# S5's order beside the input projection, and attention's values once a head

## The reference

```python
def s5_mixer(u, ...):
    lam_bar = jnp.exp(lam * dt)
    b_bar = ((lam_bar - 1.0) / lam)[..., None] * b
    bu = jnp.einsum('bsgh,gph->bsgp', uf.astype(jnp.complex64), b_bar)
    _, xs = lax.associative_scan(comb, (a, bu), axis=1)
    y = jnp.einsum('bsgp,ghp->bsgh', xs, c).real + d_skip * uf
    g = jax.nn.gelu(y)
    out = g * jax.nn.sigmoid(g @ w_glu + b_glu)

def block(args):        # attention: queries in blocks of 128, 4 heads
    s = jnp.einsum('bqhcd,bkhcd->bhcqk', qi, k) * scale
    s = jnp.where(kpos[None, :] <= qpos[:, None], s, -jnp.inf)
    p = jax.nn.softmax(s, axis=-1)
    a = p[:, :, 0] - lam * p[:, :, 1]
    return jnp.einsum('bhqk,bkhe->bqhe', a, v)
```

## Time and profile before

| | us |
|---|---|
| median of 3 runs | 1374.37 (1372.64 to 1374.88) |
| profiled execution, its own time | 1373.18 |
| its span | 1371.4 |
| TensorE busy | 1316.9 (96%) |
| TensorE weight loads busy | 1065.1 (78%) |
| VectorE busy | 849.8 (62%) |
| ScalarE busy | 500.6 (37%) |
| GpSimd busy | 612.7 (45%) |

### The profile page before, as it was taken

The page is one execution under the profiler, slowest core; times in us unless marked ns, Lnnn a source line. Parts: engine busy times, 40 slices in busy tenths (PEclk is TensorE's granted clock), DMA queues, the critical chain, the costliest instruction groups (busy, mean ns, idle before and its releaser), DMA issues.

```text
span 1371.4 us, 16028 instructions
## 1 busy us (share of the span) xinstructions
PE 1316.9 (96%) x6234; PEld 1065.1 (78%) x6234; DVE 849.8 (62%) x1149; ACT 500.6 (37%) x752; POOL 612.7 (45%) x288
## 2 busy tenths in 40 slices
PE   7988999999999999999999799989999999999999
PEld 4767777677888888888877687767778888888887
DVE  7847964656788406776237397646577771277731
ACT  5442355555323212322334234555552332122320
POOL 2966533124444444444468474312254444344442
PEclk9999999999999999999999999999999999999999
DMA  6321232013223322323233112311133333223332
GB/s 212 93 62 40 79 94 81 24 39 108 92 93 108 111 87 86 100 92 101 100 100 99 47 48 79 116 36 47 41 113 98 102 109 106 77 92 93 110 111 87
DMA packets 40939, 120.49 MB, mean 88 GB/s; under 512 B 6432, under 2 KB 10656, under 8 KB 40864
## 3 DMA queue, kind: packets, MB, share of 16 engines
q1 hardware_dynamic: 40864, 119.46, 27.3%
HBM read 114.20 MB, written 2.10 MB: 85 GB/s over the span
## 4 chain that ended last, share of the span: by engine, by line
PE 80%; DVE 9%; ACT 3%; issue 2%; SPq 2%; POOL 2%; DMA 1%; DVEq 0%; POOLq 0%; ACTq 0%
PE bank L492 25%; PE bank L505 23%; PE bank L497 23%; SPq L331 1%; PE bank L494 1%; PE bank L727 1%; PE bank L686 1%; POOL wl L353 1%; PE bank L706 1%; DVE bank L1376 1%; PE bank L716 1%; DVE xl L1137 1%; DVE G L1162 1%; ACT wh L863 1%; DMA raw<-in_w_in 1%
## 5 line engine op out<-in xcount | busy, mean ns | idle before, releaser
L353 POOL TENSOR_TENSOR wl<-raw,wh 128x1024 fp32r<-128x1024 f32 (+3 forms) x208 | 501.9, 2414 | 692.8 <-ACT wh L863 437.2
L863 ACT ACTIVATE wh<-raw 128x1024 fp32r<-128x1024 f32 (+3 forms) x208 | 218.6, 1051 | 283.9 <-PE bank L497 229.0
L492 PE MATMUL bank<-xl,wh 128*128 128x512 f32 x1152 | 308.2, 406 | 2.8 <-DVE xl L1137 2.2
L505 PE MATMUL bank<-xh,wl 128*128 128x512 f32 x1152 | 286.4, 390 | 0.0
L497 PE MATMUL bank<-xh,wh 128*128 128x512 f32 x1120 | 276.8, 389 | 0.0
L492 PEld LDWEIGHTS bank<-xl,wh 128*128 128x128 f32 x1152 | 216.7, 190 | 61.8 <-issue 12.9
L505 PEld LDWEIGHTS bank<-xh,wl 128*128 128x128 f32 x1152 | 215.4, 188 | 45.0 <-issue 0.3
L497 PEld LDWEIGHTS bank<-xh,wh 128*128 128x128 f32 x1120 | 210.2, 188 | 44.1
L1180 DVE TENSOR_TENSOR x<-x,bank 128x512 f32<-128x512 f32 x64 | 44.0, 687 | 225.3 <-PE bank L505 225.3
L492 PE MATMUL bank<-ml,wh 128*128 128x512 f32 x512 | 140.3, 402 | 0.0
L505 PE MATMUL bank<-mh,wl 128*128 128x512 f32 x512 | 127.4, 389 | 0.0
(11 more groups left out here) (292 smaller groups left out, 1271.4 us busy)
## 6 DMA issues: line engine op xcount, KB each, us to landing
raw<-in_w_gu SPq DMA_DIRECT2D x88, 512.0 KB, 3.5
raw<-in_w_in SPq DMA_DIRECT2D x52, 512.0 KB, 3.6
raw<-in_w_dn SPq DMA_DIRECT2D x32, 704.0 KB, 4.0
raw<-in_w_oe SPq DMA_DIRECT2D x16, 384.0 KB, 3.0
raw<-in_w_ol SPq DMA_DIRECT2D x16, 256.0 KB, 2.6
x<-in_x SPq DMA_DIRECT2D x8, 256.0 KB, 6.5
raw<-in_w_first SPq DMA_DIRECT2D x4, 512.0 KB, 4.8
out_x<-x SPq DMA_DIRECT2D x8, 256.0 KB, 4.5
```

The lines of the kernel that those rows point to most:

```text
L353: tt(wl[:, p, 0:cols], raw[:, p, 0:cols], wh[:, p, 0:cols].bitcast(F32), ALU.subtract).then_inc(wl_full, 1)
L492: mm(bank[b][:, :], wh[:, p, k * P:(k + 1) * P], lo[:, k, :], start=(k == 0), stop=False)
L505: w = mm(bank[b][:, :], wl[:, p, k * P:(k + 1) * P], hi[:, k, :], start=False, stop=(k == K - 1))
L863: fn(wh[:, p, 0:cols], raw[:, p, 0:cols], ACT.Copy).then_inc(wh_full, 1)
```

## The change

Units: before u (0, 1), xbc (2 to 7), z (8, 9); after z, xbc, u. S5's work follows: the input transposes in another order, the windows' copies in the tiles at MIXC of mh, without the wait for the states; the first half's input product behind unit 11, its output and the second half's input behind unit 16, the second half's output behind unit 22; VectorE's rotation and scan of a half are separate steps; GELU once for both halves at step 26. The exponentials of m2 stand behind the last SiLU. Attention: the transposed probabilities of a head are gathered by key block in `turned` (in the room of xh), and attend(h) makes four products, key block k with all queries from block k on; scores(n) is one product for each softmax.

The diff, cut to its core:

```diff
+        turned = [sb(f"turned{i}", [P, NQ, T], at=offsets["xh"] + i * NQ * T * 4) for i in range(2)]
-        local = [sb(f"s5_local{i}", [P, 4, P], at=offsets[n]) for i, n in enumerate(("bmat", "cf"))]
+        local = [sb(f"s5_local{i}", [P, 4, P], at=offsets["mh"] + (MIXC + i) * T * 4) for i in range(2)]
...
-                if s == 5:
-                    sp.wait_ge(unit_out, unit_out_of(l, 1))
-                if 5 <= s <= 8:
+                if 11 <= s <= 14:
+                    i = (s - 11) // 2
+                    if s % 2:
+                        sp.wait_ge(unit_out, unit_out_of(l, 8 + i))
...
-                if s in (17, 18, 21, 22):
+                if s in (20, 21, 25, 26):
...
-                    if 6 <= s <= 7:
-                        table(l, 0, s - 6)
-                    if 8 <= s <= 11:
-                        for n in ((0,), (1, 2), (3,), (4, 5))[s - 8]:
+                    if 6 <= s <= 8:
+                        state_terms(l, s - 6)
+                    if 9 <= s <= 10:
+                        table(l, 0, s - 9)
+                    if 11 <= s <= 12:
+                        for n in ((3, 4), (5,))[s - 11]:
                             state_terms(l, n)
...
             def s5_windows(l, i):
                 pe.wait_ge(kernels_copied, l + 1)
-                if i:
-                    pe.wait_ge(states_ready, 2 * (l + 1))
                 claim(6, local_copied)
...
-                if q:
-                    for c, b in enumerate(banks):
-                        mm(bank[b][:, 0:q * P], qs[c], qk[rows[c], 2 * h + 1, 0:q * P], start=True, stop=True)
                 for c, b in enumerate(banks):
-                    mm(bank[b][:, last], qs[c], qk[rows[c], 2 * h + 1, last], start=True, stop=False)
+                    w = (q + 1) * P
+                    mm(bank[b][:, 0:w], qs[c], qk[rows[c], 2 * h + 1, 0:w], start=True, stop=False)
...
-            def attend(l, n):
-                h, q = n // NQ, n % NQ
+            def attend(l, h):
...
-                pe.wait_ge(probs_turned, nth(probs_turned))
-                for k in range(q + 1):
-                    w = mm(bank[5][:, q * P:(q + 1) * P], v[:, k, h * P:(h + 1) * P],
-                           G[:, 4 + n % 2, k * P:(k + 1) * P], start=(k == 0), stop=(k == q))
+                pe.wait_ge(probs_turned, nth(probs_turned, NQ))
+                for k in range(NQ):
+                    w = mm(bank[5][:, k * P:], v[:, k, h * P:(h + 1) * P], turned[h % 2][:, k, k * P:],
+                           start=(k == 0), stop=(k == NQ - 1))
...
-                    if n:
-                        attend(l, n - 1)
+                    if n and n % NQ == 0:
+                        attend(l, n // NQ - 1)
...
-                attend(l, STEPS - 1)
+                attend(l, HEADS - 1)
...
                 for s in range(1, NIN):
                     prep()
+                    if 7 <= s <= 10:
+                        s5_inputs((1, 2, 4, 5)[s - 7])
...
+                    if s in (17, 23):
+                        y_copy((s - 17) // 6)
...
-                    if s in (20, 24):
-                        gelu((s - 20) // 4)
+                    if s == 26:
+                        gelu(0)
+                        gelu(1)
+                        ln_exp_tables()
...
-                        s5_scan(l, 0)
...
+                        s5_rotate(l, 0, 0)
+                        s5_rotate(l, 0, 1)
...
-                        s5_scan(l, 1)
+                        s5_scan(l, 0)
...
-                        s5_back(l, 1)
+                        s5_back(l, 0)
...
+                    if 17 <= s <= 18:
+                        s5_rotate(l, 1, s - 17)
+                    if 19 <= s <= 20:
+                        s5_scan(l, 1, [s - 19])
+                    if s == 21:
+                        s5_back(l, 1)
+                    if s in (21, 25):
+                        s5_finish(l, (s - 21) // 4)
...
-    order = [w[:, :, s5:z], w[:, :, xbc:dt], w[:, :, z:xbc], w[:, :, sc + 256:sc + 512], w[:, :, sc + 512:s5],
+    order = [w[:, :, z:xbc], w[:, :, xbc:dt], w[:, :, s5:z], w[:, :, sc + 256:sc + 512], w[:, :, sc + 512:s5],
```

More of the change, by code:

```diff
@@ L764, in _ @@
                         dt_turn()
[L765 to L766 removed]
+                    if s in (6, 8):
+                        s5_inputs(l, (0, 3)[(s - 6) // 2])
                     if s == 7:
@@ L791, in _ @@
                         m2_decays(3)
+                    if s == 16:
                         s5_out(l, 0)
-                    if s == 16:
+                        s5_in(l, 1)
                         m2_norm()
[L795 to L798, removed]
                     if 17 <= s <= 24:
@@ L970, in _ @@
                     prep()
[L971 to L975, removed]
+                    if 7 <= s <= 10:
+                        s5_inputs((1, 2, 4, 5)[s - 7])
+                    if s == 11:
+                        for i in range(2):
+                            s5_weights(local[i][:].rearrange("p a b -> p (a b)"), bank[6][:, :], local_copied)
+                    if s in (15, 21):
+                        s5_copy((s - 15) // 6)
+                    if s in (17, 23):
+                        y_copy((s - 17) // 6)
                     if s == 2:
@@ L986, in _ @@
                         fn(s16[:, 7, :], s16[:, 5, :], ACT.Exp).then_inc(decay_exp, 1)
[L987 to L991, removed]
+                    if l == 0 and s == 9:
+                        act.wait_ge(lam_go, 1)
+                        fn(lam2[:, :, :], lam2[:, :, :], ACT.Exp).then_inc(lam_exp, 1)
+                    if s == 10:
                         m2_head(0)
@@ L1348, in lambda_factors, with s5_rotate, s5_scan @@
                 own(tt(mlam_all[:, :], mlam_all[:, :], pre[:, :, PRE["linit"]].rearrange("p a b -> p (a b)"), SUB))
-            a5, c5, e5 = [t[:, :] for t in (sA, sC, sE)]
-            def s5_scan(l, j):
+            a5, c5, e5 = [t[:, :] for t in (sA, sE, sE)]
+            def s5_rotate(l, j, part):
                 cs, sn = [t[:, :] for t in tab[j]]
-                dve.wait_ge(tab_full, nth(tab_full))
-                dve.wait_ge(dve_bank[2], nth(dve_bank[2]))
-                dve.wait_ge(dve_bank[3], nth(dve_bank[3]))
-                if l or j:
-                    dve.wait_ge(s5x_ready, 2 * l + j)
-                re, im = bank[2][:, :], bank[3][:, :]
-                own(tt(a5, re, cs, MUL))
-                own(tt(c5, im, cs, MUL))
-                dve.wait_ge(dve_own, owned() - 1)
-                own(tt(re, re, sn, MUL))
-                dve.wait_ge(dve_own, owned() - 1)
-                own(tt(im, im, sn, MUL))
-                dve.wait_ge(dve_own, owned() - 1)
-                own(tt(re, c5, re, SUB))
-                dve.wait_ge(dve_own, owned() - 1)
-                own(tt(im, a5, im, ADD))
-                for back, rows in ((1, re), (0, im)):
-                    dve.wait_ge(dve_own, owned() - back)
+                re, im = bank[2][:, :], bank[3][:, :]
+                if part == 0:
+                    dve.wait_ge(tab_full, nth(tab_full))
+                    dve.wait_ge(dve_bank[2], nth(dve_bank[2]))
+                    dve.wait_ge(dve_bank[3], nth(dve_bank[3]))
+                    if l or j:
+                        dve.wait_ge(s5x_ready, 2 * l + j)
+                    own(tt(a5, re, cs, MUL))
+                    own(tt(c5, im, cs, MUL))
+                    dve.wait_ge(dve_own, owned() - 1)
+                    own(tt(re, re, sn, MUL))
+                else:
+                    dve.wait_ge(dve_own, owned())
+                    own(tt(im, im, sn, MUL))
+                    own(tt(re, c5, re, SUB))
+                    dve.wait_ge(dve_own, owned() - 1)
+                    own(tt(im, a5, im, ADD))
+            def s5_scan(l, j, parts=(0, 1)):
+                re, im = bank[2][:, :], bank[3][:, :]
+                for rows in [(re, im)[k] for k in parts]:
+                    dve.wait_ge(dve_own, owned())
                     for k in range(4):
@@ L1554, in _ @@
                 for i in range(2):
-                    scaled(u[:, i, :].rearrange("p (t c) -> p c t", t=CH), i, "p (c t) -> p c t", t=CH)
+                    scaled(z[:, i, :], i)
                 dt_scaled()
@@ L1574, in _ @@
                         lambdas()
-                    if l == 0 and s == 9:
+                    if l == 0 and s == 10:
                         lambda_factors()
@@ L1578, in _ @@
                         m2_sums()
-                    if s == 7:
+                    if 8 <= s <= 9:
+                        i = s - 8
+                        scaled(u[:, i, :].rearrange("p (t c) -> p c t", t=CH), i, "p (c t) -> p c t", t=CH)
+                    if s == 8:
                         m2_weights()
@@ L1600, in _ @@
                         m2_mix(1)
-                        s5_back(l, 0)
+                        s5_rotate(l, 0, 0)
+                        s5_rotate(l, 0, 1)
                     if 12 <= s <= 13:
```

92 lines of the change are left out of this document (40 added, 52 removed).

## The result

| | before | after |
|---|---|---|
| median us (4 runs each) | 1374.11 (1372.64 to 1374.88) | 1352.83 (1350.01 to 1354.09) |
| profiled execution, own time / span | 1373.18 / 1371.4 | 1352.78 / 1350.8 |
| TensorE busy | 1316.9 (96%) | 1310.9 (97%) |

Ratio 0.9851, 95% interval 0.9839 to 0.9864: 21 us faster, where 26.6 were forecast (1347.8 from 1374.4); 1352.83 lies in the range. First the chain by engine and TensorE's waits in total, as in the earlier trace rows.

The account below looks back on a forecast made before the run. TensorE was taken to bound the kernel, so only its work and gaps count. 1373.2 - 30.5 (input projection) + 3.9 (y copies) + 0 (attention) = 1346.6 us, 1347.8 against the median of 1374.4; range 1339 to 1359 for 8 in 10.

Parts of the forecast that it names:

- L574: S5's windows, input projection: dropping the wait for the states removes 11.5 us of waits and 5.3 of slow clock, 16.8 us.
- L551 and L562: S5's input transposes and kernels: reordered ScalarE copies remove 13.1 us of waits and about 3 of slow clock, 16 us.
- The vector chain: Units 11 to 16: VectorE becomes late, 2 us at second m2_apply and 0.8 at s5_out(0) a layer, 5.6 us added.
- A in all: First S5 transposes to start of unit 17: 30.5 us booked as removed, including 3.3 us beyond the named gaps.
- The y copies: Units 17 to 27: copies delay partner rows, 3.8 us a layer added, 3.7 us relief; net 3.9 us added.
- Attention, 0: Attention: wider value products and moved cover cancel to 0 a layer, bounds -1.5 and +2.5 us.
- SP's chunk copies at nothing: Loads of units 12 to 15: 32 DMAs copying u into chunks delay them, costed at nothing because the double buffer covers.
- the vector chain's clock at the y gap: Vector-chain rival: 2.8 + 4 us more, the y gap's lower clock adding 2 to 3; 1355 us, chance 0.17.
- the free y copies: Rival, units 17 to 27: partner rows arrive in time or copies go faster; -7.6 us, 1340 us, chance 0.12.
- the surviving wait: Rival, S5's windows: the wait is for local_copied or bank 6 and stays; +16.8 us, 1365 us, chance 0.04.
- the wide products: Rival, attention values: wide products are cheaper by the Trainium skill's rule, 10.7 us in all; 1337 us, chance 0.02.
- the slow SP: Rival: chunk copies hold up loads of units 12 to 15, 39.5 us over two layers; 1387 us, chance 0.04.

Follow-up runs that it names:

- windows_free: Kernel before with only the wait of S5's second window for the states removed, copies and the rotation's second buffer placed elsewhere: ratio 0.9868, 1354.08 us.
- copy_first: Changed kernel with ScalarE's copy of S5's input group 0 moved ahead of the SiLU of step 6: ratio 0.9867, 1354.73 us.
- all_five: Changed kernel with the edits of y_last_gelu26, vector_cover, attn_split and copy_first, plus VectorE's constant work of layer 0 moved out of step 3: ratio 0.9691, 1329.15 us.
- vector_cover: Changed kernel with second m2_apply behind unit 15, VectorE's s5_back(0) ahead of the second sc tile's low half, norm's sums ahead of s5_out(0): 0.9821, 1347.74 us.
- chunks_16: Changed kernel with the 32 copies of u into chunks in two batches of sixteen instead of four of eight: ratio 0.9888, 1357.76 us.
- y_last_gelu26: Changed kernel with y's second-half DMAs behind tile 7's partner rows and the last S5 sum a step later, GELUs kept at step 26: 0.9784, 1342.50 us.
- attn_narrow: Changed kernel with a head's values as ten products of 128 columns instead of four wide ones, same place: ratio 0.9864, 1353.47 us.
- attn_split: Changed kernel with the values of the first and of the last head each computed in two parts at different places: ratio 0.9826, 1348.13 us.
- attn_alone: Kernel before with the change to attention alone: ratio 1.0009, 1374.38 us.
- y_last: Changed kernel with y's second-half DMAs behind tile 7's partner rows, and the last S5 sum and both GELUs one step later: ratio 0.9851, 1352.54 us.

## Why the prediction was right, and where not

- **L574, 16.8 us: right, a little large.** windows_free gave 18, of which some 16 lie at the wait and behind it.
- **L551 and L562, 16 us: right but for one wait.** 13.1 us of waits became 2.0, in layer 0 alone. I named the third group as tightest; it was the first, held up by a convolution that VectorE did late. copy_first and all_five show the cause, some 7 us of constant work in step 3: without it, in all_five, the wait is gone. I had followed ScalarE's order with before's durations, and not asked when VectorE would be ready for its SiLU.
- **The vector chain, 5.6 us added: right in sum.** Measured 1.21 and 1.22 us at the second m2_apply (2 a layer booked, 1.7 worked out) and 1.36 and 1.37 at s5_out (0.8 booked): 5.2 us. vector_cover shows that the order makes them, not the load.
- **A in all: 28.1 us against 30.5.** The surviving wait is 2.0 of the 2.4 us, the term of L574 0.8; the vector chain cost 0.4 less than booked.
- **The y copies: the mechanism right, the price too low.** The gap is 3.31 us (3.3 forecast), at the turn of v 0.4 in layer 1 alone (0.5 a layer). Without them B is 5.2 and 5.8 us shorter, not 3.8: 1.6 us of the difference is the slow clock behind the gap (5.66 and 5.65 us for two parts that take 4.07 without it). I had it in a rival, 2 to 3 us in all, and left it out of the forecast, though the earlier trace rows show it behind both long gaps. The relief of 3.7 us came: without the gap B is 71.67 and 71.64 us against 73.06 and 73.62, 3.4 us. Net +7.6 against +3.9: this is 3.7 of the 6.0 us by which the profiled spans miss the sum, A 2.4 and attention 1.1. The 1.2 us that the rest of the kernel came out shorter are luck.
- **Attention, 0: mis-sized by 0.9 us a layer,** within its bounds (-1.5 to +2.5). The width was right (0.6 us). The term that failed is the wait of 1.23 us for VectorE at the last head's turns, which the third head's products were to fill: 0.59 us of it is left in both layers. The new wait at the last head's products (0.78 us) is near the 0.67 booked.
- **SP's chunk copies at nothing: right as placed,** but the cover that I named was TensorE's. chunks_16 shows that the first to pay is ScalarE's queue.
- Of the rivals, the vector chain's clock at the y gap was a part of the truth; the free y copies, the surviving wait, the wide products and the slow SP are refuted by y_last_gelu26, windows_free, attn_narrow and the profile of after, in which TensorE waits for no weights from the first S5 transposes to the last head's sum. The price of the vector rival left out its own last term: 1347.8 + 6.8 is the 1355 told, and with 2 to 3 us for the clock it is 1357.

## What to carry to other kernels

Price a new gap on TensorE with the slow part behind it, read from such a part in the same trace: here 1.6 us behind one of 3.3. When a transfer or a table load moves, ask of each in-order engine what is queued behind the instruction that waits for it; the first to be late is often not the one for whom the load is meant. And before a large reordering try the one wait that the profile puts first: here its removal alone gave 18 us, where the whole change gave 21.

## What the runs showed that I had not expected

- Waits of 1.9 and 1.3 us, close together, go with a low granted clock too: 0.68 and 0.58 over the 11 to 12 us from the end of the first, and 0.83 and 0.70 where products stand in the second of them. So of the 2.7 us a layer that attn_split won, 1.6 are idle time and the rest clock.
- The same code's stretch C varies by 1.5 us between the layers of one execution (73.30 and 74.76 in after) with nearly the same idle time (5.8 and 5.6 us): the clock again, 0.95 and 0.93 in the mean. Stretch A does it too: with the S5 code of before, it takes 100.33 and 93.38 us in before, 98.98 and 94.99 in attn_alone. Differences under 1.5 us in a stretch need several profiles.
- ScalarE's table load takes 1.28 us in the rows of y_last, and the next operation starts at once, so two loads cost 2.6 us. The Trainium skill (ScalarE: Activation LUTs, "What ACT_TABLE_LOAD costs") has the same 1.28 us for the load, and another 1.38 us for draining at each switch, of which these rows show nothing.
